# Layer 1's attention with V as the stationary operand and both heads in one bank

## The chip, the cores and the metric

The kernel runs on one core of one Trainium2 chip. The metric is the device time of one execution in microseconds. TensorE is called PE below, VectorE DVE, ScalarE ACT, GpSimdE POOL, SyncE SP (it issues the DMAs).

## The reference

A trunk of two layers on 1024 tokens of 1024 channels, in float32. Layer 0 is differential attention beside a pooling mixer, layer 1 a gated short convolution beside dilated attention; each is followed by a SwiGLU feed-forward block. The change touches layer 1's attention alone. It has 8 heads of 64 channels and three branches of a window and a dilation, whose outputs are combined by their softmax denominators:

```
D_BRANCHES = ((128, 1), (512, 4), (2048, 16))
s = q k^T * 64**-0.5 - slope * distance     # -inf outside window, dilation, causality
o_branch = softmax(s) v ;  lse_branch = m + log(den)
o = sum over branches of softmax(lse)[branch] * o_branch
x = x + concat([conv_part, o]) @ w_out
```

The combined output is the same as one softmax in which a key that lies in several branches counts as often, so the kernel adds one table (the log of the count, or a large negative number) and takes one softmax.

## The kernel before

**Units and tiles.** Layer 1's attention works in 4 units of two heads (m = 0, 1), each over 8 query tiles of 128 tokens (i = 0 to 7), 32 tiles in all, counted by n. Tile i has i + 1 blocks of 128 keys. Per tile and head: PE scores the queries against the keys (`score`, two float32r matmuls for each 512 keys, into PSUM banks 0 and 1 for head 0, 2 and 3 for head 1); DVE adds the bias table while it moves the scores to SBUF, and takes the minimum of the negated sums (`biased`, line 2440); ACT takes the exponential and its sum, the denominator DEN (line 1798); PE transposes the exponentials block by block (`turn`, line 1162) into banks 4 to 6 in turn; ACT copies the first four blocks of the turned map to SBUF and DVE the rest (`turned`, lines 1589 and 2561); PE multiplies the turned map with V (`weigh`, line 1181) into bank 7; DVE multiplies by the reciprocal of the denominator (`denominator`, line 2566, and `scaled`, line 2573) into Y.

In `weigh` the turned map's block (128 keys x 128 queries) is the stationary operand and V's block (128 keys x 64 columns) is moved. The output has 128 queries as partitions and 64 columns. Both heads use the same 64 columns of bank 7, one after the other. The operands are plain float32; most other matmuls are float32r.

**Order.** Each engine has its own instruction list, written out by hand, with semaphores between the lists. For tile n PE runs: turn of head 0, score of head 0 for tile n + 2, weigh of head 0 for tile n - 1, then the same three for head 1. A score waits until DVE has reduced the tile before it in the same banks (`s_mx`), a turn until ACT has taken the exponential (`s_ex`) and a bank of 4 to 6 is free, a weighing until the turned map is copied (`t_ea`, `t_ed`) and bank 7 is free (`o_ok`). DVE runs for tile n: reciprocal of head 0 of tile n - 1, `biased` of head 0 for tile n + 1, reciprocal of head 1, `scaled` of head 1 of tile n - 2, `biased` of head 1, the copy of head 0's turned map, `scaled` of head 0 of tile n - 1, the copy of head 1's turned map. At i = 6 it also builds the two bias tables of the next unit (line 2424).

**After attention.** Y (tokens as partitions) must be turned for the output projection: `turn_y` makes 8 transposes for each of the 4 units (line 1366). They stand between the projection's first tiles (`u_tile`, lines 1083 to 1085, the convolution's half of the channels); ACT and DVE then split the turned Y into high and low float32r parts (`y_hi`, `y_lo`). SP loads three further pieces of the output weights once the last weighing is done (line 805); ACT and DVE split them (`split_o`).

Of the kernel before, what the change touches and what calls it, by code (L numbers as in the profile page):

```python
# [82 lines left out]
def trunk(nc, a, out):  # L83
    ctx = ExitStack()
    with ctx:
# [23 lines left out]
        Y = at("Y", [P, NT, HALF], F32, oA)  # L109
        WOh = at("WOh", [P, 2, D], F32R, oV)  # L110
# [175 lines left out]
        YJ = at("YJ", [P, P], F32, oK + 4 * KB)  # L286

# [75 lines left out]
        o_pe = [sems("o_peA"), sems("o_peB")]  # L363
        o_ok = [sems("o_okA"), sems("o_okB")]
# [90 lines left out]
        def weighed(L, m, n):  # L455

            return bank(7 if n < FILL_FROM and n % 2 else 6)[:, 0:P] if L == 0 else bank(7)[:, 0:HD]
# [128 lines left out]
        def _(sp):  # L586
# [13 lines left out]
            for L in range(2):  # L600
# [479 lines left out]
        def _(pe):  # L1080
# [85 lines left out]
            def weigh(L, m, n):  # L1166

                u, i = n // NT, n % NT
                if n == 0:
                    pe.wait_ge(bank_free[L], 3 * NT)  # L1170
                pe.wait_ge(t_ea[m][L], n + 1)
                if L == 1 and i >= 4:
                    pe.wait_ge(t_ed[m][1], 4 * u + i - 3)
                if L == 0:
                    pe.wait_ge(o_ok[0][0], n + (1 if n < FILL_FROM else 2))
                else:
                    pe.wait_ge(o_ok[1 - m][1], n + 2 + m)
                w, off = (P, u * P) if L == 0 else (HD, u * P + HD * m)
                turned = PTL[m][i % 2] if L else PT[i % 2]
                for j in range(i + 1):  # L1180
                    last = pe.matmul(weighed(L, m, n), turned[:, P * j:P * j + P], V[:, j, off:off + w],  # L1181
                                     start=(j == 0), stop=(j == i))
                last.then_inc(o_pe[m][L], 1)


            for L in range(2):
                for f in (ja_free if L == 0 else []) + [s_mx[0][L], s_mx[1][L]]:
                    pe.sem_inc(f, 1)
                for f in (t_pe[0][L], t_pe[1][L], o_ok[0][L], o_ok[1][L]):
                    pe.sem_inc(f, 2)  # L1190
                pe.sem_inc(od_add[L], 4)
                pe.sem_inc(bank_free[L], NT)
            pe.wait_ge(idn_ok, 4)
            for L in range(2):
# [135 lines left out]
                def out_block(n):  # L1330

                    q, t = n // NT, n % NT
                    if n == 0:
                        pe.wait_ge(uh_lo, 4)

                        pe.wait_ge(o_ok[0][0], 1 + FILL_FROM)
# [7 lines left out]
                    elif n == BLOCKS_IN + 2:  # L1344
                        pe.wait_ge(o_ok[0][0], 2 + TILES0)
# [7 lines left out]
                def turn_y(j):  # L1353
                    if L == 0:
                        pe.wait_ge(y_ok, j + 1)
                        if j < 2:

                            for m in range(2):
                                pe.wait_ge(s_mx[m][0], 1 + TILES0)
                    else:  # L1360
                        pe.wait_ge(o_ok[0][1], 2 + 8 * UNITS)
                        pe.wait_ge(o_ok[1][1], 2 + 8 * UNITS)
                    if j >= 2:
                        pe.wait_ge(yt_lo, 4 * L + j - 1)
# [4 lines left out]
                if L == 0:  # L1369
                    for u in range(UNITS):  # L1370
                        b, g = u % 2, NT * u
                        following = stacks_before(0, u + 1)
                        for i in range(NT):
# [9 lines left out]
                            if g + i > 0:  # L1383
                                weigh(0, 0, g + i - 1)
# [8 lines left out]
                    weigh(0, 0, TILES0 - 1)  # L1393
                else:
                    for u in range(UNITS):
                        b, g = u % 2, NT * u
                        following = stacks_before(1, u + 1)
                        for i in range(NT):
# [3 lines left out]
                            turn(1, 0, u, i)  # L1402
                            if i == NT - 2 and more:
# [5 lines left out]
                            if g + i > 0:  # L1409
                                weigh(1, 0, g + i - 1)  # L1410
# [5 lines left out]
                            if g + i > 0:  # L1416
                                weigh(1, 1, g + i - 1)
                    for m in range(2):
                        weigh(1, m, TILES0 - 1)
# [6 lines left out]
                else:  # L1426
                    pe.wait_ge(uh_lo, 8)
                    pe.wait_ge(wo_lo, WO_AT[1] + 1)
                    for t in range(NT):
                        if t == 1:  # L1430
                            for m in range(2):
                                pe.wait_ge(o_ok[m][1], 2 + TILES0)
# [151 lines left out]
        def _(act):  # L1584
# [124 lines left out]
            for L in range(2):  # L1709
# [135 lines left out]
                def split_o(g):  # L1845
# [3 lines left out]
                    elif g == 1:  # L1849
                        for m in range(2):  # L1850
                            act.wait_ge(o_pe[m][1], 8 * UNITS)
# [13 lines left out]
                def turned(m, g, i):  # L1865
                    act.wait_ge(t_pe[m][L], g + i + 3)
                    if L == 0:
                        if g + i >= 2:
                            act.wait_ge(o_pe[0][0], g + i - 1)
                        w = P * (i + 1)  # L1870
                        src, to = PS[:, 4 * HALF:4 * HALF + w], PT[i % 2]
                    else:
                        w = min(HALF, P * (i + 1))
                        if g + i >= 2:
                            act.wait_ge(o_pe[m][1], g + i - 1)
# [5 lines left out]
                def scaled(n):  # L1881
# [3 lines left out]
                    act.wait_ge(o_pe[0][0], n + 1)  # L1885
                    act.wait_ge(o_ok[0][0], n + 2)
                    nc.scalar.activation(YJ[:], weighed(0, 0, n), ACT.Square, scale=RDN[:, c:c + 1],
                                         accum_out=YSS[:, n:n + 1]).then_inc(y_sq, 1)
                    copy(Y[:, i, P * u:P * u + P], weighed(0, 0, n), scale=RDN[:, c:c + 1]).then_inc(o_ok[0][0], 1)

                def y_hi(j):
                    act.wait_ge(yt_pe, 4 * L + j + 1)
                    kw = dict(scale=SUBG[:, 0:1]) if L == 0 else {}
                    copy(HH[:, (0, 4)[L] + j, :], PS[:, 1024 * (j % 2):1024 * (j % 2) + 1024], **kw).then_inc(yt_hi, 1)
# [8 lines left out]
                if L == 0:  # L1903
                    for n in range(TILES0):
# [15 lines left out]
                        elif n == 12:  # L1920
                            act.wait_ge(o_pe[0][0], NT)
# [208 lines left out]
        def _(dve):  # L2130
# [196 lines left out]
            for L in range(2):  # L2327
# [177 lines left out]
                def y_lo(j):  # L2505
                    dve.wait_ge(yt_hi, 4 * L + j + 1)
                    src, c = PS[:, 1024 * (j % 2):1024 * (j % 2) + 1024], (0, 4)[L] + j
                    if L == 0:
# [4 lines left out]
                        else:  # L2513
                            dve.wait_ge(o_pe[0][0], TILES0 + j - 3)
# [5 lines left out]
                def unit_scaled(u):  # L2520

                    dve.wait_ge(y_rs, u + 1)
                    dve.wait_ge(o_ok[0][0], 2 + NT * (u + 1))
# [4 lines left out]
                if L == 0:  # L2528
                    for n in range(TILES0):
# [11 lines left out]
                        if n >= 4:  # L2541
                            dve.wait_ge(o_ok[0][0], n - 1)
# [10 lines left out]
                else:  # L2553
                    def turned(m, n):
                        u, i = n // NT, n % NT
                        if i >= 4:
                            dve.wait_ge(t_pe[m][1], n + 3)
                            dve.wait_ge(o_pe[m][1], n - 1)
# [16 lines left out]
                    for n in range(TILES0):  # L2575
# [8 lines left out]
                        if n > 0:  # L2584
                            denominator(0, n - 1)
# [13 lines left out]
                        if n > 0:  # L2599
                            scaled(0, n - 1)  # L2600
# [3 lines left out]
                    denominator(0, TILES0 - 1)  # L2604
                    scaled(1, TILES0 - 2)
                    scaled(0, TILES0 - 1)
                    denominator(1, TILES0 - 1)
                    scaled(1, TILES0 - 1)
# [258 lines left out]
```

## Time and profile before

| what | us |
|---|---|
| median of 3 runs | 2194.12 |
| lowest and highest | 2192.97, 2194.75 |
| the profiled execution's span, first to last instruction | 2193.9 |
| layer 1's attention, from its first matmuls to the output projection, counted from the span's start | 1317 to 1455 |
| one of its four units | 33.88 |

The span is the time of the profiled execution from its first to its last instruction; it lies within the three timed runs, and no other time of that execution is given. Times inside it count from its start. In a timeline a row can hold several instructions of the same kind in a row (x10); its length then runs from the start of the first to the modelled end of the last, and the start of the next row shows when the engine could take the next one. A PE pass's modelled end lies well after the start of the pass behind it, since passes overlap.

### The profile page before, as it was taken

To read this page: it belongs to the slowest core of one execution; us is meant where nothing else is said; L and a number is where in the kernel's file an instruction comes from. 1 tells how busy PE (TensorE), PEld (TensorE's weight loads), DVE (VectorE), ACT (ScalarE), POOL (GpSimd) and SP (SyncE) were. 2 spreads that over 40 slices of the span, in tenths; PEclk is the share of its full clock that TensorE was granted. 3 is DMA by queue.
4 is the path that set the end of the run, shared out by engine and by line. 5 is a ranking of instruction groups with operands and counts; after the bars stand their busy time and mean duration, and the time that the engine had idled before them with its cause. 6 is when DMAs were issued, how large, how long until landed. Compare 5 with 4: busy or idle time off the path is not lost.

```text
span 2193.9 us, 30208 instructions
## 1 busy us (share of the span) xinstructions
PE 2156.8 (98%) x10572; PEld 1809.3 (82%) x10572; DVE 1323.6 (60%) x1829; ACT 900.8 (41%) x1497; POOL 860.1 (39%) x563
## 2 busy tenths in 40 slices
PE   8999999999999999999999999999999999999999
PEld 7877798888888887888888888988888888887887
DVE  4345875765555555558597356656765555555555
ACT  4134874443333334435332148642433333334433
POOL 1022442466666672002244133220466777652000
PEclk9999999999999999999999999999999999999999
DMA  5011421055555448674312111311155555557665
GB/s 190 7 59 41 125 78 30 20 183 201 193 190 167 155 152 285 193 244 155 115 39 58 49 58 40 116 39 39 54 195 184 187 179 170 172 172 273 194 195 192
DMA packets 229536, 295.56 MB, mean 135 GB/s; under 512 B 11825, under 2 KB 133169, under 8 KB 229169
## 3 DMA queue, kind: packets, MB, share of 16 engines
q1 hardware_dynamic: 229136, 294.04, 41.0%
q8 instruction: 68, 1.11, 0.2%
q14 instruction: 44, 0.35, 0.1%
q10 hardware_dynamic: 288, 0.05, 0.0%
HBM read 208.06 MB, written 77.59 MB: 130 GB/s over the span
## 4 chain that ended last, share of the span: by engine, by line
PE 81%; issue 13%; DVE 2%; ACT 2%; POOL 2%; DMA 1%; SPq 0%; POOLq 0%; DVEq 0%; ACTq 0%
PE PS L1533 12%; PE PS L1532 12%; PE PS L1531 12%; PE PS L1558 6%; PE PS L1559 6%; PE PS L1560 6%; PE PS L1181 4%; PE PS L1083 4%; PE PS L1085 4%; PE PS L1084 4%; PE PS L1162 2%; POOL QRS L989 1%; PE PS L1137 1%; PE PS L1138 1%; PE PS L1248 1%
## 5 line engine op out<-in xcount | busy, mean ns | idle before, releaser
L2136 DVE TENSOR_TENSOR LINEl<-LINE,HIGH 128x1024 fp32r<-128x1024 f32 x154 | 195.1, 1274 | 167.5 <-ACT HIGH L1589 167.1
L1589 ACT ACTIVATE HIGH<-LINE 128x1024 fp32r<-128x1024 f32 x154 | 163.0, 1060 | 235.8 <-PE PS L1560 209.9
L1558 PE MATMUL PS<-HIGH 128*128 128x512 f32 x616 | 240.3, 390 | 4.4 <-ACT KEEP L1589 4.0
L1560 PE MATMUL PS<-HIGH,LINEl 128*128 128x512 f32 x616 | 239.7, 389 | 0.0
L1559 PE MATMUL PS<-LINEl,HIGH 128*128 128x512 f32 x616 | 239.6, 389 | 0.0
L2136 DVE TENSOR_TENSOR SLOTl<-BLOCKS,RING 128x512 fp32r<-128x512 f32 x168 | 156.0, 929 | 95.3 <-ACT RING L1589 90.7
L921 POOL TENSOR_TENSOR ST<-ST 128x512 f32<-128x512 f32 x132 | 192.5, 1459 | 32.4 <-DMA ST<-in_ffn_w_down 23.8
L1589 ACT ACTIVATE RING<-BLOCKS 128x512 fp32r<-128x512 f32 x168 | 105.9, 630 | 227.2 <-PE PS L1533 223.1
L2136 DVE TENSOR_TENSOR SLOTl<-SLOT,RING 128x512 fp32r<-128x512 f32 x126 | 132.7, 1053 | 88.1 <-ACT RING L1589 87.9
L1558 PEld LDWEIGHTS PS<-HIGH 128*128 128x128 f32 x616 | 115.6, 188 | 29.5 <-DVE LINEl L2136 2.9
L989 POOL TENSOR_TENSOR QRS<-QMS,EXPO 128x8 f32<-128x8 f32 x32 | 52.1, 1638 | 220.8 <-DVE QMS L2397 220.2
L1560 PEld LDWEIGHTS PS<-HIGH,LINEl 128*128 128x128 f32 x616 | 115.6, 188 | 23.9
L1559 PEld LDWEIGHTS PS<-LINEl,HIGH 128*128 128x128 f32 x616 | 115.7, 188 | 23.8
L1589 ACT ACTIVATE RING<-SLOT 128x512 fp32r<-128x512 f32 x126 | 79.2, 630 | 125.5 <-PE PS L1533 115.2
L1531 PE MATMUL PS<-B1h,RING 128*128 128x512 f32 x336 | 130.7, 389 | 0.0
L1532 PE MATMUL PS<-B1l,RING 128*128 128x512 f32 x336 | 130.7, 389 | 0.0
L1533 PE MATMUL PS<-B1h,SLOTl 128*128 128x512 f32 x336 | 130.7, 389 | 0.0
L893 POOL TENSOR_TENSOR SLOT<-BLOCKS 128x512 f32<-128x512 f32 x42 | 55.3, 1316 | 189.8 <-DMA BLOCKS<-in_ffn_w_up 189.8
L926 POOL TENSOR_TENSOR RST<-MSQ,EXPO 128x1 f32<-128x1 f32 x32 | 22.8, 714 | 233.9 <-DVE MSQ L2154 233.9
L1083 PE MATMUL PS<-WQh,HH 128*128 128x512 f32 x256 | 102.5, 400 | 0.6 <-DVE U L2449 0.6
L1085 PE MATMUL PS<-WQh,HL 128*128 128x512 f32 x256 | 99.9, 390 | 0.0
L1084 PE MATMUL PS<-WQl,HH 128*128 128x512 f32 x256 | 99.7, 389 | 0.0
(418 smaller groups left out, 5807.1 us busy)
## 6 DMA issues: line engine op xcount, KB each, us to landing
LINE<-hidden SPq DMA_DIRECT2D x154, 256.0 KB, 2.7
hidden<-HID SPq DMA_DIRECT2D x44, 512.0 KB, 4.4
ST<-in_ffn_w_down SPq DMA_DIRECT2D x44, 512.0 KB, 4.1
sums<-ST SPq DMA_DIRECT2D x22, 1024.0 KB, 6.2
hidden<-ST SPq DMA_DIRECT2D x22, 1024.0 KB, 6.7
LINE<-sums SPq DMA_DIRECT2D x88, 256.0 KB, 2.9
BLOCKS<-in_ffn_w_gate SPq DMA_DIRECT2D x42, 512.0 KB, 4.0
BLOCKS<-in_ffn_w_up SPq DMA_DIRECT2D x42, 512.0 KB, 5.3
```

Of the source, the lines that this page charges most:

```text
L921: nc.gpsimd.tensor_tensor(dst, x, y, op).then_inc(st_sum, 1)
L1083: pe.matmul(dst, lh, rh, start=first, stop=False)
L1084: pe.matmul(dst, lh, rl, start=False, stop=False)
L1085: return pe.matmul(dst, ll, rh, start=False, stop=last)
L1531: pe.matmul(dst, lh, rh[:, k, :], start=k == 0 and not adds_on, stop=False, skip_group_check=adds_on)
L1532: pe.matmul(dst, lh, rl[:, k, :], start=False, stop=False, skip_group_check=adds_on)
L1533: last = pe.matmul(dst, ll, rh[:, k, :], start=False, stop=k == 3, skip_group_check=adds_on)
L1558: pe.matmul(dst, hi[:, 0, ts], hi[:, 1, :], start=j == 0 and not adds_on, stop=False, skip_group_check=adds_on)
L1559: pe.matmul(dst, hi[:, 0, ts], lo[:, 1, :], start=False, stop=False, skip_group_check=adds_on)
L1560: pe.matmul(dst, lo[:, 0, ts], hi[:, 1, :], start=False, stop=j == NJ - 1, skip_group_check=adds_on).then_inc(dn_pe, 1)
L1589: return nc.scalar.activation(dst, src, ACT.Copy, **kw)
L2136: return v.tensor_tensor(dst, src, hi.bitcast(F32), ALU.subtract)
```

## The change

V's block becomes the stationary operand (64 columns) and the turned map is moved (128 queries), so the output has the 64 channels as partitions and 128 queries as columns. Head 0 writes partitions 0 to 63 and head 1 partitions 64 to 127 of the same 128 columns of bank 7; the two heads' matmuls alternate block by block in one function, `weigh_unit`, which stands where head 0's weighing stood. The output is then already turned as the projection needs it: it goes to YT, and layer 1's `turn_y` is gone. The denominators, which belong to queries and so now to columns, must be turned too: DVE takes the reciprocals of both heads' denominators, each repeated over 64 columns (`denominators_by`, 128 x 128 into RB), PE transposes that (`turn_by`, into bank 7's next 128 columns), DVE copies it to SBUF (RS) and multiplies the weighed output by it (`unit_scaled_out`). Semaphores of the two heads' weighings become one. Layer 0 keeps its computation; its functions only lose the argument for the layer.

```diff
+        YT = at("YT", [P, UNITS, TOK], F32, oA)
+        RB = [at(f"RB{b}", [P, P], F32, oK + 4 * KB + 512 * b) for b in range(2)]
+        RS = [at(f"RS{b}", [P, P], F32, oK + 5 * KB + 512 * b) for b in range(2)]
...
+        def unit_out():
+            return bank(7)[:, 0:P]
+        def unit_by():
+            return bank(7)[:, P:2 * P]
...
-                    for m in range(2):
-                        sp.wait_ge(o_pe[m][1], TILES0)
+                    sp.wait_ge(o_pe[1], TILES0)
...
-            def weigh(L, m, n):
...
-                w, off = (P, u * P) if L == 0 else (HD, u * P + HD * m)
-                turned = PTL[m][i % 2] if L else PT[i % 2]
-                for j in range(i + 1):
-                    last = pe.matmul(weighed(L, m, n), turned[:, P * j:P * j + P], V[:, j, off:off + w],
-                                     start=(j == 0), stop=(j == i))
-                last.then_inc(o_pe[m][L], 1)
+            def turn_by(n):
+                if n == 0:
+                    pe.wait_ge(bank_free[1], 3 * NT)
+                pe.wait_ge(o_ok[1], n + 2)
+                pe.wait_ge(rb_ok, n + 1)
+                pe.transpose(unit_by(), RB[n % 2][:], IDN[:])
+
+            def weigh_unit(n):
+                u, i = n // NT, n % NT
+                for m in range(2):
+                    pe.wait_ge(t_ea[m][1], n + 1)
+                    if i >= 4:
+                        pe.wait_ge(t_ed[m][1], 4 * u + i - 3)
+                for j in range(i + 1):
+                    for m in range(2):
+                        off = u * P + HD * m
+                        last = pe.matmul(unit_out()[HD * m:HD * m + HD, :], V[:, j, off:off + HD],
+                                         PTL[m][i % 2][:, P * j:P * j + P], start=(j == 0), stop=(j == i))
+                last.then_inc(o_pe[1], 1)
...
                             turn(1, 0, u, i)
+                            if g + i > 0:
+                                turn_by(g + i - 1)
...
                                 score(1, 0, b, g, i + 2)
                             if g + i > 0:
-                                weigh(1, 0, g + i - 1)
+                                weigh_unit(g + i - 1)
                             turn(1, 1, u, i)
...
                                 score(1, 1, b, g, i + 2)
-                            if g + i > 0:
-                                weigh(1, 1, g + i - 1)
-                    for m in range(2):
-                        weigh(1, m, TILES0 - 1)
+                    turn_by(TILES0 - 1)
+                    weigh_unit(TILES0 - 1)
...
                         u_tile(0, t)
-                        if t in (1, 3, 5, 7):
-                            turn_y(t // 2)
...
                 def y_hi(j):
+                        act.wait_ge(o_ok[1], 2 + NT * (j + 1))
+                        copy(HH[:, 4 + j, :], YT[:, j, :]).then_inc(yt_hi, 1)
...
-                    def denominator(m, n):
-                        c = m + 2 * (n % 2)
-                        dve.wait_ge(s_ex[m][1], n + 1)
-                        att.did(v.reciprocal(RDN[:, c:c + 1], DEN[:, c:c + 1]))
-
-                    def scaled(m, n):
+                    def denominators_by(n):
+                        c = 2 * (n % 2)
+                        for m in range(2):
+                            dve.wait_ge(s_ex[m][1], n + 1)
+                        by = DEN[:, c:c + 2].rearrange("p (m o) -> p m o", o=1).broadcast_to([P, 2, HD])
+                        v.reciprocal(RB[n % 2][:].rearrange("p (m d) -> p m d", d=HD), by).then_inc(rb_ok, 1)
+
+                    def unit_scaled_out(n):
                         u, i = n // NT, n % NT
-                        c, off = m + 2 * (n % 2), u * P + HD * m
-                        att.wait()
-                        dve.wait_ge(o_pe[m][1], n + 1)
-                        v.tensor_scalar(Y[:, i, off:off + HD], weighed(1, m, n), RDN[:, c:c + 1], None, ALU.mult).then_inc(o_ok[m][1], 1)
+                        dve.wait_ge(o_pe[1], n + 1)
+                        att.link(v.tensor_copy(RS[n % 2][:], unit_by()))
+                        v.tensor_tensor(YT[:, u, P * i:P * i + P], unit_out(), RS[n % 2][:], ALU.mult).then_inc(o_ok[1], 1)
...
                         if n > 0:
-                            denominator(0, n - 1)
+                            denominators_by(n - 1)
                         if i == NT - 1:
                             att.wait()
                         if more:
                             biased(0, b, g, i + 1)
-                        if n > 0:
-                            denominator(1, n - 1)
-                        if n > 1:
-                            scaled(1, n - 2)
-                        if more:
                             biased(1, b, g, i + 1)
                         turned(0, n)
...
                         if n > 0:
-                            scaled(0, n - 1)
+                            unit_scaled_out(n - 1)
                         turned(1, n)
```

## Rows read from the trace of the kernel before

**Rows 1.** The page, busy time: us, share of the span, instructions.

```profile
PE 2156.8 (98%) x10572; PEld 1809.3 (82%) x10572; DVE 1323.6 (60%) x1829; ACT 900.8 (41%) x1497; POOL 860.1 (39%) x563
```

**Rows 2.** Busy time by stretch: a unit, the end of attention, the projection's start.

```profile
core 0: us, PE busy (x) PEld busy (x) DVE busy (x) ACT busy (x) POOL busy (x), PEclk, DMA share, GB/s
1349.92:1383.80 33.88, 32.97 (x265) 30.89 (x265) 22.62 (x75) 24.41 (x55) 9.86 (x6) 1.00 0.14 32
...
1452.00:1456.00 4.00, 3.81 (x18) 3.71 (x19) 0.39 (x3) 0.00 (x0) 0.00 (x0) 0.60 0.00 0
1456.00:1460.00 4.00, 4.00 (x11) 3.09 (x10) 0.69 (x1) 0.00 (x0) 0.00 (x0) 0.55 0.75 262
1455.05:1482.61 27.56, 27.56 (x130) 22.89 (x130) 16.38 (x21) 5.00 (x4) 0.00 (x0) 0.92 0.22 77
```

**Rows 3.** Timeline of PE over head 0 of one tile (start, length, instructions).

```profile
1366.98 0.82 PE L1162 MATMUL PS<-IDN,PR 128*128 128x128 f32 x6
1367.56 0.48 PE L1137 MATMUL PS<-K,QST 128*128 128x512 f32 x1
...
1368.57 1.22 PE L1181 MATMUL PS<-V,PT 128*128 128x64 f32 x10
1369.63 0.83 PE L1162 MATMUL PS<-IDN,PR 128*128 128x128 f32 x6
```

**Rows 4.** Instructions of three lines: ns of one, minimum, median and maximum.

```profile
L1277 PE MATMUL PS<-U,PW x16: 591/592/595, 156.5 to 167.9; 128*128 128x512 f32 x16
...
L1366 PE MATMUL PS<-IDN,Y x64: 270/272/273, 346.2 to 1482.6; 128*128 128x128 f32 x64
...
L1181 PE MATMUL PS<-V,PTB x320: 217/275/423, 1323.3 to 1454.9; 128*128 128x64 f32 x160
```

**Rows 5.** Timeline of DVE behind the weighing of Rows 3.

```profile
1369.90 0.28 DVE L2573 TENSOR_SCALAR Y<-PS,RDN 128x64 f32<-128x64 f32 x1 [1.02 <-PE PS L1181]
1370.49 0.42 DVE L2561 COPY PTB<-PS 128x256 f32<-128x256 f32 x1 [0.30 <-PE PS L1162]
1370.83 0.15 DVE L2566 RECIPROCAL RDN<-DEN 128x1 f32<-128x1 f32 x1
1370.90 1.21 DVE L2440 CUSTOM_DVE_ANT_0 PR<-PS,BIAS 128x1024 f32<-128x1024 f32 x1
1372.03 0.09 DVE L2440 DVE_READ_ACCUMULATOR2_ANT NMX<- 128x1 f32 x1
```

**Rows 6.** Instructions of two lines: the reciprocals, of one and two columns.

```profile
L2566 DVE RECIPROCAL RDN<-DEN x64: 152/158/163, 1318.7 to 1452.0; 128x1 f32<-128x1 f32 x64
...
L2482 DVE RECIPROCAL RDN<-DEN x32: 156/160/167, 215.8 to 341.3; 128x2 f32<-128x2 f32 x32
```

**Rows 7.** Groups by line, DVE in the unit of Rows 2: busy us, mean ns, idle before.

```profile
L2573 DVE TENSOR_SCALAR Y<-PS,RDN 128x64 f32<-128x64 f32 x16 | 4.5, 284 | 10.4 <-PE PS L1181 10.3
L2424 DVE SCALAR_TENSOR_TENSOR BIAS<-DIST,SM,MASK 128x1024 f32<-128x1024 f32 x2 | 2.9, 1436 | 0.0
...
L2561 DVE COPY PTB<-PS 128x512 f32<-128x512 f32 x2 | 1.4, 692 | 0.5 <-PE PS L1162 0.5
...
L2561 DVE COPY PT<-PS 128x128 f32<-128x128 f32 x2 | 0.6, 286 | 0.0
L2440 DVE CUSTOM_DVE_ANT_0 PR<-PS,BIAS 128x128 f32<-128x128 f32 x2 | 0.6, 285 | 0.0
```

**Rows 8.** Timeline: a hand-over from DVE to a waiting PE.

```profile
1317.42 0.69 DVE L2418 TENSOR_TENSOR QN<-PS,QRS 128x512 f32<-128x512 f32 x1 [0.72 <-POOL QRS L989]
...
1318.16 0.66 PE L1268 MATMUL PS<-IDN,QN 128*128 128x128 f32 x4 [0.70 <-DVE QN L2418]
```

**Rows 9.** Timeline of PE at the end of attention.

```profile
1446.58 1.04 PE L1162 MATMUL PS<-IDN,PR 128*128 128x128 f32 x8
...
1449.67 1.97 PE L1181 MATMUL PS<-V,PTB 128*128 128x64 f32 x16 [0.54 <-DVE Y L2573]
1452.18 3.11 PE L1181 MATMUL PS<-V,PTB 128*128 128x64 f32 x16 [0.54 <-DVE Y L2573]
```

More of the change, by code:

```diff
@@ L453, in turn_bank, with weighed @@
             return bank(4 + c) if L == 0 else bank(4 + TURNS.index((m, i, c)) % 3)
-        def weighed(L, m, n):
-            return bank(7 if n < FILL_FROM and n % 2 else 6)[:, 0:P] if L == 0 else bank(7)[:, 0:HD]
+        def weighed(n):
+            return bank(7 if n < FILL_FROM and n % 2 else 6)[:, 0:P]
+        def unit_out():
+            return bank(7)[:, 0:P]
+        def unit_by():
+            return bank(7)[:, P:2 * P]
         def block_out(n):
@@ L1164, in turn, with weigh @@
                 last.then_inc(t_pe[m][L], 1)
-            def weigh(L, m, n):
+            def weigh(n):
                 u, i = n // NT, n % NT
                 if n == 0:
[L1170 to L1177, printed above, removed]
-                w, off = (P, u * P) if L == 0 else (HD, u * P + HD * m)
-                turned = PTL[m][i % 2] if L else PT[i % 2]
+                    pe.wait_ge(bank_free[0], 3 * NT)
+                pe.wait_ge(t_ea[0][0], n + 1)
+                pe.wait_ge(o_ok[0], n + (1 if n < FILL_FROM else 2))
                 for j in range(i + 1):
-                    last = pe.matmul(weighed(L, m, n), turned[:, P * j:P * j + P], V[:, j, off:off + w],
+                    last = pe.matmul(weighed(n), PT[i % 2][:, P * j:P * j + P], V[:, j, u * P:u * P + P],
                                      start=(j == 0), stop=(j == i))
-                last.then_inc(o_pe[m][L], 1)
+                last.then_inc(o_pe[0], 1)
+            def turn_by(n):
[16 more added lines that the diff above has]
+                last.then_inc(o_pe[1], 1)
             for L in range(2):
@@ L1188, in _ @@
                     pe.sem_inc(f, 1)
-                for f in (t_pe[0][L], t_pe[1][L], o_ok[0][L], o_ok[1][L]):
+                for f in (t_pe[0][L], t_pe[1][L], o_ok[L]):
                     pe.sem_inc(f, 2)
@@ L1392, in _ @@
                     turn_y(1)
-                    weigh(0, 0, TILES0 - 1)
+                    weigh(TILES0 - 1)
                 else:
@@ L1430, in _ @@
                         if t == 1:
-                            for m in range(2):
-                                pe.wait_ge(o_ok[m][1], 2 + TILES0)
+                            pe.wait_ge(o_ok[1], 2 + TILES0)
                         u_tile(0, t)
-                        if t in (1, 3, 5, 7):
-                            turn_y(t // 2)
                     pe.wait_ge(wo_lo, WO_AT[1] + 2)
@@ L1849, in split_o @@
                     elif g == 1:
-                        for m in range(2):
-                            act.wait_ge(o_pe[m][1], 8 * UNITS)
+                        act.wait_ge(o_pe[1], TILES0)
                     else:
@@ L1884, in scaled @@
                     c = 2 * (i % 4)
[L1885 to L1887 removed]
+                    act.wait_ge(o_pe[0], n + 1)
+                    act.wait_ge(o_ok[0], n + 2)
+                    nc.scalar.activation(YJ[:], weighed(n), ACT.Square, scale=RDN[:, c:c + 1],
                                          accum_out=YSS[:, n:n + 1]).then_inc(y_sq, 1)
[L1889 removed]
+                    copy(Y[:, i, P * u:P * u + P], weighed(n), scale=RDN[:, c:c + 1]).then_inc(o_ok[0], 1)
                 def y_hi(j):
[L1892 to L1894 removed]
+                    if L == 0:
+                        act.wait_ge(yt_pe, j + 1)
+                        copy(HH[:, j, :], PS[:, 1024 * (j % 2):1024 * (j % 2) + 1024], scale=SUBG[:, 0:1]).then_inc(yt_hi, 1)
+                    else:
+                        act.wait_ge(o_ok[1], 2 + NT * (j + 1))
+                        copy(HH[:, 4 + j, :], YT[:, j, :]).then_inc(yt_hi, 1)
                 def score_done():
@@ L2603, in _ @@
                             next_bias(1)
[L2604 to L2608, printed above, removed]
+                    denominators_by(TILES0 - 1)
+                    unit_scaled_out(TILES0 - 1)
                 def split_o(g):
```

41 lines of the change are left out of this document (19 added, 22 removed).

## The prediction

> **What bounds the kernel now.** I read the page's busy times first: PE is busy 98% of the span [rows 1]. Then the busy time by stretch, on layer 1's attention and what follows it: one unit (two heads, eight query tiles) takes 33.88 us, in which PE is busy 32.97, ACT 24.41 and DVE 22.62 [rows 2]. So PE sets the pace of this stage, and the others have about 10 us of room in each unit. Then PE's timeline over one tile [rows 3]: six transposes hold PE 0.58 us, a 1024-key score of one head 1.01 us (0.126 per 128 keys), and the weighing of a tile with five key blocks ten passes in 1.06 us. A plain f32 matmul is thus two passes on the array, and with V's 64 columns moved each pass takes 0.106 to 0.108 us. One unit has 36 blocks for each of two heads, 144 passes, 15.5 us: almost half of PE's time there.
>
> Is that pass bound by moving columns or by loading weights? Another f32 matmul moves 512 columns in passes of 592 ns [rows 4]; a transpose of 128 columns reads 272 ns and a weighing pass of 64 at the least 217, so a moved column costs (592 - 272) / 384 = 0.83 ns, 0.106 us for 128 columns and 0.053 for 64. The old pass moves 64 columns and takes 0.108: it waits for its 128 columns of weights. The new pass loads 64 and moves 128, so it is 0.106 by its moving columns. **Turning the operands round alone gains nothing**; the gain must come from the two halves of the array working at the same time.
>
> **The change part by part.**
>
> *Weighing.* 72 matmuls a unit stay 72, with 144 passes of 0.106. If head 1's passes run beside head 0's, a key block of both heads takes 0.213 us and a unit 7.7 us; if not, 15.3. No row shows two 64-column matmuls side by side, so these are the two ends. I take 7.7, since the two heads alternate block by block and use different partitions of the bank. PE then has 15.5 - 7.7 = 7.8 us a unit less, and one transpose a tile more (eight, 0.9 us): 33.9 would become about 27 if nothing else held it.
>
> *What takes its place: a loop through DVE.* The tile after next can't be scored for head 0 until DVE has reduced the one before it (one pair of PSUM banks per head), PE issues that score ahead of the weighing, and DVE reaches that reduction only after it has scaled the previous tile's weighed output. So weighing, scaling, the copy of the second half of head 1's turned map, the reciprocal, the reduction, the score and the next weighing form a chain that repeats once a tile. Both kernels have it. Before, per unit: hand-over to DVE 0.27 (from PE's next start at 1369.63 to DVE's at 1369.90) x 8 = 2.2; scaling 0.20 x 8 = 1.6 (0.28 less the overlap of 0.08 that successive DVE rows show); copies 1.6 (four, 0.49 on the mean, less overlap) and 0.7 of waits for their transposes; reciprocal 0.07 x 8 = 0.6; reductions 5.3 (0.285 to 1.21 us, mean 0.75, less overlap, x 8); reading the minimum and hand-over to PE (0.09 + 0.05) x 8 = 1.1; scores 36 x 0.126 = 4.5; weighing of head 0 7.7; one bias table 1.2: 26.5 of 33.9 us, hidden under PE [rows 2, 3, 5, 6, 7, 8]. DVE's 10.4 us of waits for weighing are that room [rows 7].
>
> After, per unit:
> - Scaling becomes a copy of the turned reciprocals out of PSUM (128x128, 0.286 by the copy's row), its own hand-over (0.05, as from DVE to PE [rows 8]) and a product (0.29 less 0.08): 0.55 x 8 = 4.4, that is +2.8.
> - The reciprocal of one column becomes one of 128 columns, 64 repeated twice. No row shows a wide reciprocal. At the copy's slope, (692 - 286) / 384 = 1.06 ns per element, it is 0.157 + 127 x 1.06 = 0.29 us. The rows of one and of two columns [rows 6] differ by 3 ns in the mean: 0.54 us. At the most they differ by 15 ns (152 to 167): 2.06 us. I take 0.86 us, 5.5 ns per element, between the mean and the middle of the extremes (7.5), since the mean stands on a single added element: (0.86 - 0.08) x 8 = 6.2, that is +5.6. The ends are 1.7 and 15.8.
> - Switching the array between whole and halves, twice a tile. Below: nothing. Above: the pass in flight must end first, 0.272 - 0.108 = 0.16, and the next be started, 0.05 (as after DVE). I take half, 0.1, for each of eight entries and, through the later transposes, for half of the exits: +1.2 (ends 0 and 2.4).
> - The bias tables of the next unit, 1.44 us each, fall into two neighbouring tiles. The second stays on the chain (1.2); the first now runs longer than the short score and weighing that it runs beside (about 2.9 us of DVE work against 1.7): +1.1.
>
> Sum: 26.5 + 2.8 + 5.6 + 1.2 + 1.1 = 37.2 us a unit against 33.9. The chain is then longer than PE's 27 and sets the pace: +3.3 x 4 = **+13.2 us**.
>
> The page TensorEngine Tiling (Array Packing) of the Trainium skill (section Key Properties) says that a change of tiling mode drains TensorE. By it the switch is at its upper end, the chain 1.2 longer, and the time 5 us more; no row here shows a switch. Half of the chance of the forecast's case lies on that side.
>
> *The end of attention.* Before, from the last transposes to the start of the second part of the output projection: 1446.58 to 1482.61, 36.0 us [rows 2, 9]. In it head 0's and head 1's last weighings follow each other with waits of 0.54, the granted clock is 0.60 and 0.55 in the two stretches from 1452 to 1460 (it falls from 2.4 to 1.2 GHz there, after those waits), and the 32 transposes of Y (3.5) stand between the projection's tiles. The projection's 96 matmuls alone are 27.56 - 3.5 - 2.2 (the half clock) = 21.9. After: transposes 0.86, hand-over and copy 0.27 + 0.69, reciprocal 0.86, its turn 0.1, one weighing 1.7 to 1.9, 4.8 in all; then 21.9; and DVE, which frees the projection's banks, has y_lo(0) and split_o(1) in front (3072 elements at 1.06, 3.2 us) without PE's transposes to cover them: I count half, 1.6. Together 28.3, 7.7 less; if the clock falls as before (3 us) 4.7. I take **-6.3**. y_hi no longer waits for PE; SP's three loads and their waits keep their order, and nothing is queued behind a new wait there. PE's new waits (for the reciprocal, for bank 7) have behind them the score and the weighing, which is the chain above. ACT needs 24.4 us a unit and stays hidden.
>
> Sum: 2193.9 (the profiled span, inside the three runs of 2192.97 to 2194.75, median 2194.12) + 13.2 - 6.3 = **2201 us**.
>
> **The rivals.**
> 1. *The wide reciprocal is as cheap as a copy* (0.29 to 0.45 us) and the switch is free. For it: other DVE rows grow by about 1 ns per element. Then the unit is 37.2 - 4.5 - 1.2 = 31.5 us, -9.6 in four, and the end gives 8: 2176, up to 2187 with 0.45 us and some switching. It decides below 0.5 us of reciprocal. This is the case that ends faster.
> 2. *The halves don't overlap*, or 64 columns of weights load no faster than 128: the change doesn't do what it says. Weighing is 15.3 us a unit and lies on the chain: 37.2 + 7.6 = 44.8, +44 in four, 2232; with the cheap reciprocal 2214. Against it only the issue order speaks.
> 3. *The reciprocal costs at least 7.5 ns per element*, the middle of the extremes: 1.11 us or more, +2 us a unit and +8 in all, 2209 to 2215. For it: the extremes lean upwards. Against it: the mean of 3 ns.
>
> The page VectorE: DVE Perf Modes of the Trainium skill (section First, the fixed hardware budget) says that a reciprocal divides iteratively with a repeat count of 8. By eight times the copy's slope an estimate is 1.22 us and the time 2212: this rival. The 3 ns of our rows don't agree with it, but they are one element.
>
> **How the numbers follow.** About 0.2%, 4.4 us, is what these runs can tell from no change. Chances: the forecast's case 0.33 (own range 2190 to 2212: 0.03 faster, 0.12 within, 0.18 slower), rival 1 0.29, rival 2 0.24, rival 3 0.14. Faster 0.29 + 0.03 = 0.32; same 0.12; slower 0.18 + 0.24 + 0.14 = 0.56. The range 2176 to 2234 goes from rival 1's lower end to just past rival 2's upper one, and leaves out longer reciprocals together with halves that don't overlap.
>
> **What would show it.** The weighing's sixteen pass pairs of a last tile should start 1.7 us apart from first to last (3.4 would be rival 2). The reciprocal's row should read 0.86 us (0.3: rival 1; over 1.1: rival 3). DVE's waits for weighing should shrink from 10.4 us a unit while PE shows idle time before its scores or its turn of the reciprocals, and PE's busy share of the unit should fall well below 32.97 of 33.88. A unit should take about 37 us. The forecast is wrong if the chain is not the one that PE waits for (ACT's copies instead), or if PE, now idle in every tile, is granted the lower clock inside attention: 12 us of scores and weighings a unit would then double.

## The result, and the profile after

The changed kernel takes 2204.81 us (median of 4 runs, 2202.9 to 2206.96) against 2193.55 (2192.46 to 2194.75): ratio 1.005, 95% interval 1.0036 to 1.0064, 11 us slower. The forecast was 2201, slower. The profiled execution has a span of 2201.1 us (its own time is 2202.9, so 1.8 us lie around the span), 7.2 more than before's 2193.9.

The page's busy times, answering to [rows 1], show little: PE works 17 us less and DVE 20 more.

```profile
PE 2140.1 (97%) x10572; PEld 1775.0 (81%) x10572; DVE 1343.7 (61%) x1797; ACT 902.2 (41%) x1497; POOL 861.0 (39%) x563
```

The busy time by stretch, for the unit that answers to the one of [rows 2]:

```profile
core 0: us, PE busy (x) PEld busy (x) DVE busy (x) ACT busy (x) POOL busy (x), PEclk, DMA share, GB/s
...
1355.02:1392.84 37.82, 30.71 (x273) 24.00 (x272) 27.98 (x66) 24.75 (x55) 9.87 (x6) 1.00 0.12 29
```

A unit takes 37.82 us where it took 33.88. PE was busy in all but 0.9 us of a unit; now it is idle for 7.1, and no engine fills the unit. That is what a loop through several engines looks like. The waits of PE and of DVE in that unit name its two ends (total, times, longest):

```profile
PE PS L1195 <- DVE RB L2589: 4.7, 4, 2.0
PE PS L1148 <- DVE NMX L2461: 2.2, 5, 0.7
```

```profile
DVE RS L2594 <- PE PS L1207: 8.9, 7, 2.3
DVE PTB L2582 <- PE PS L1173: 0.6, 2, 0.4
```

PE waits for the reciprocal (`turn_by`, L1195) and for the reductions (`score`, L1148), and DVE waits for the weighing (L1207). DVE's groups by line in the same unit, answering to [rows 6, 7]:

```profile
L2589 DVE RECIPROCAL RB<-DEN 128x128 f32<-128x128 f32 x8 | 7.5, 942 | 0.0
...
L2595 DVE TENSOR_TENSOR YT<-PS,RS 128x128 f32<-128x128 f32 x8 | 2.3, 291 | 0.3
L2594 DVE COPY RS<-PS 128x128 f32<-128x128 f32 x8 | 2.3, 290 | 8.9 <-PE PS L1207 8.9
```

One turn of the loop can be read off the two timelines. First DVE, answering to [rows 5] (the weighed tile is scaled, and the same for the next tile at 1377.65):

```profile
1372.31 0.29 DVE L2594 COPY RS<-PS 128x128 f32<-128x128 f32 x1 [1.13 <-PE PS L1207]
1372.64 0.29 DVE L2595 TENSOR_TENSOR YT<-PS,RS 128x128 f32<-128x128 f32 x1
1373.00 0.29 DVE L2582 COPY PT<-PS 128x128 f32<-128x128 f32 x1
1373.21 0.94 DVE L2589 RECIPROCAL RB<-DEN 128x128 f32<-128x128 f32 x1
1374.07 1.03 DVE L2461 CUSTOM_DVE_ANT_0 PR<-PS,BIAS 128x896 f32<-128x896 f32 x1
1375.02 0.08 DVE L2461 DVE_READ_ACCUMULATOR2_ANT NMX<- 128x1 f32 x1
...
1377.65 0.29 DVE L2594 COPY RS<-PS 128x128 f32<-128x128 f32 x1 [1.20 <-PE PS L1207]
```

Then PE, answering to [rows 3]:

```profile
1374.30 0.30 PE L1195 MATMUL PS<-IDN,RB 128*128 128x128 f32 x1
1375.16 0.50 PE L1148 MATMUL PS<-K,QST 128*128 128x512 f32 x1 [0.56 <-DVE NMX L2461]
1375.49 0.40 PE L1149 MATMUL PS<-K,QST 128*128 128x512 f32 x1
1375.73 0.40 PE L1148 MATMUL PS<-K,QST 128*128 128x512 f32 x1
1375.96 0.40 PE L1149 MATMUL PS<-K,QST 128*128 128x512 f32 x1
1376.29 1.31 PE L1207 MATMUL PS<-PT,V 128*64 128x128 f32 x20
1377.53 0.88 PE L1173 MATMUL PS<-IDN,PR 128*128 128x128 f32 x6
```

From 1372.31: scaling and a wait for the next transposes 0.69, copy 0.21, reciprocal 0.86, reduction with its minimum about 1.03, hand-over to PE 0.06, score 1.13, weighing 1.24, hand-over to DVE 0.12: 5.34 us, and at 1377.65 it begins anew. Every step starts when the one before it ends. The two weighings of this turn start 5.12 us apart; before, the same two started 4.63 apart (the second is in [rows 3], the first of each pair here, after and before):

```profile
1371.17 1.09 PE L1207 MATMUL PS<-PTB,V 128*64 128x128 f32 x16
```

```profile
1363.94 1.00 PE L1181 MATMUL PS<-V,PTB 128*128 128x64 f32 x8
```

The end of attention, PE's timeline from the last transposes, answering to [rows 9]:

```profile
1462.10 1.09 PE L1173 MATMUL PS<-IDN,PR 128*128 128x128 f32 x8
1464.92 0.30 PE L1195 MATMUL PS<-IDN,RB 128*128 128x128 f32 x1 [1.73 <-DVE RB L2589]
1465.16 1.97 PE L1207 MATMUL PS<-PTB,V 128*64 128x128 f32 x32
1467.06 0.50 PE L1094 MATMUL PS<-WOh,UH 128*128 128x512 f32 x1
...
1479.52 0.50 PE L1094 MATMUL PS<-WOh,UH 128*128 128x512 f32 x1 [1.26 <-DVE X L2346]
...
1490.53 0.39 PE L1094 MATMUL PS<-WOh,UH 128*128 128x512 f32 x1
```

From the last transposes to the projection's second part (1490.53) are 28.4 us; before they were 36.0.

**Where the 7.2 us of the span come from.** From the first score (at 1314.3 before) to the last transposes 132.3 us became 148.9 (+16.6: the middle units +3.9 each, the stretch up to the first unit's last weighing +6.2, the last unit's part +2.6). The end gives 7.6 back (3.2 of them by the clock, below), the projection's second part 0.8. The rest is spread: the first score starts 1.1 us earlier, although nothing was changed ahead of it. Such differences between executions are not the change's: over the runs below, the identical part behind the projection's first half takes from 687.9 to 691.3 us. So the verdicts below go by ratios and by the length of a unit, not by single spans.

**The clock.** In the +6.2 of the first unit a stretch shows a lower granted clock (by stretch, the columns as above; the first row is the stretch before):

```profile
1346.00:1349.00 3.00, 1.35 (x15) 1.24 (x17) 2.47 (x7) 1.03 (x4) 0.00 (x0) 0.92 0.00 0
1349.00:1352.00 3.00, 3.00 (x25) 2.67 (x22) 0.58 (x2) 0.00 (x0) 0.00 (x0) 0.51 0.00 0
```

The same weighing there, and one unit later:

```profile
1348.15 2.95 PE L1207 MATMUL PS<-PT,V 128*64 128x128 f32 x28
...
1387.59 1.75 PE L1207 MATMUL PS<-PT,V 128*64 128x128 f32 x28
```

After a stretch in which PE was busy for 1.35 of 3.00 us the clock is at 1.2 GHz for some 3 us. From that weighing to the next are 6.87 us instead of 5.25: 1.6 us. Such a stretch does not always lower the clock: in the next two units and at the end of attention PE is busy for 1.40, 1.09 and 1.27 of 3.00 us (from 1385.50, 1423.00 and 1462.00), and the clock stays at 1.00. What decides it is not shown.

The profiled execution of the kernel before has a dip too, at the end of attention [rows 2]. Experiment 4 below has the same end without a dip, and there the stretch from the last transposes to the projection's second part (1457.19 to 1489.97) takes 32.8 us instead of 36.0. So 3.2 of the 7.6 us that the end gives back are the clock of one execution, and 4.4 the change's own. The profiled execution of the changed kernel is the one of the four with the highest mean clock (0.999 and 2202.9 us; the others 0.997 and 0.998, 2204.7 to 2207.0). So more such dips in the other executions would account for the median's lying 1.9 above it; there is no trace of them, so this is argued, not shown.

### The profile page after: what moved, and what is told of

Same layout as the page of the kernel before. It is cut to its first block, busy times and chain, and to the rows that moved or that the text cites. A ratio compares the mean times of both kernels' runs of the same rounds, so it can differ in the third digit from the quotient of the medians.

```text
span 2201.1 us, 30153 instructions
## 1 busy us (share of the span) xinstructions
PE 2140.1 (97%) x10572; PEld 1775.0 (81%) x10572; DVE 1343.7 (61%) x1797; ACT 902.2 (41%) x1497; POOL 861.0 (39%) x563
## 3 DMA queue, kind: packets, MB, share of 16 engines
q8 instruction: 68, 1.11, 0.2%
## 4 chain that ended last, share of the span: by engine, by line
PE 77%; issue 13%; DVE 4%; ACT 2%; POOL 2%; DMA 1%; SPq 0%; POOLq 0%; DVEq 0%; ACTq 0%
PE PS L1551 12%; PE PS L1552 12%; PE PS L1550 12%; PE PS L1577 6%; PE PS L1578 6%; PE PS L1579 6%; PE PS L1094 4%; PE PS L1096 4%; PE PS L1095 4%; PE PS L1207 1%; POOL QRS L1000 1%; PE PS L1274 1%; PE PS L1272 1%; PE PS L1273 1%; PE PS L1148 1%
## 5 line engine op out<-in xcount | busy, mean ns | idle before, releaser
L1817 ACT ACTIVATE PR<-PR,NMX 128x256 f32<-128x256 f32 (+7 forms) x128 | 98.5, 774 | 9.4 <-DVE NMX L2461 9.1
```

The source lines that it names most:

```text
L1817: nc.scalar.activation(pr, pr, ACT.Exp, bias=NMX[:, c:c + 1], scale=-1.0, accum_out=DEN[:, c:c + 1]).then_inc(s_ex[m][L], 1)
```

## The experiments

They ran on three chips (1 to 4, 5 to 8, and 9 and 10), each time beside the kernel before, whose median there was 2195.4 to 2196.4. Times are given as ratios to it; the changed kernel's is 1.005.

**1. The reciprocal of two columns**, spread over the partitions by PE.

```diff
-                pe.transpose(unit_by(), RB[n % 2][:], IDN[:])
+                c = 2 * (n % 2)
+                for m in range(2):
+                    pe.matmul(unit_by()[HD * m:HD * m + HD, :], RDN[:, c + m:c + m + 1].broadcast_to([P, HD]), IDN[:], start=True, stop=True)
...
-                        v.reciprocal(RB[n % 2][:].rearrange("p (m d) -> p m d", d=HD), by).then_inc(rb_ok, 1)
+                        v.reciprocal(RDN[:, c:c + 2], DEN[:, c:c + 2]).then_inc(rb_ok, 1)
```

> The reciprocal takes two columns instead of 128; PE spreads each over 64 partitions by reading the column 64 times as stationary operand. Loop theory (every DVE instruction between the scaling and head 0's next reduction is added to each tile): the reciprocal falls from 0.94 to about 0.16 us, 0.78 less for each of 8 tiles, so a unit falls from 37.8 to about 31.6 us and the kernel by 25 us, to about 2180 (2177 to 2186, PE's own 29 to 30 us a unit being the floor). Rival (PE itself needs the 37.8 us: switching between whole and halves, and the clock): within 3 us of the changed kernel's 2204.8. Rival (DVE's total work is the bound, 28.0 us busy a unit plus hand-overs): also about 2180.

Measured: 2192.75 us, ratio 0.999 (0.9981 to 1.0), 13 us less than the changed kernel, half of what was expected; a unit 34.21 us where about 31.6 was expected. The busy time of that unit and PE's two waits in it:

```profile
1387.28:1421.49 34.21, 31.74 (x298) 24.62 (x297) 22.84 (x66) 24.56 (x54) 9.89 (x6) 1.00 0.40 128
```

```profile
1416.05 0.44 PE L1197 MATMUL PS<-IDN,RDN 128*64 128x128 f32 x4 [1.76 <-DVE RDN L2590]
...
1420.57 0.44 PE L1197 MATMUL PS<-IDN,RDN 128*64 128x128 f32 x4 [0.60 <-DVE RDN L2590]
```

The reciprocal was on the loop: 0.27 to 0.75 us came off in seven of the eight tiles. But then PE's own 31.7 us show, and 2.4 us of waits in the two tiles where DVE builds the next unit's bias tables. The rival that PE needs 37.8 falls.

**2. One head after the other** in the weighing.

```diff
-                for j in range(i + 1):
-                    for m in range(2):
+                for m in range(2):
+                    for j in range(i + 1):
```

> All of head 0's matmuls of a weighing first, then all of head 1's; the work is the same. If two neighbouring matmuls of different halves run at the same time, as the passes 0.055 us apart suggest, the overlap is lost: a weighing of eight blocks takes 3.5 us instead of 1.97, a unit 7.6 us more, the kernel 30 us more, about 2235. Rival (a pass with 64 columns of weights is short by itself, whichever half the one before used): no change, 2205.

Measured: 2221.15 us, ratio 1.0116 (1.0099 to 1.0132), 14 us more than the changed kernel; a unit 42.13 us, 4.3 more. PE's weighings of eight blocks (with what follows), of two and of four:

```profile
1400.41 3.33 PE L1207 MATMUL PS<-PTB,V 128*64 128x128 f32 x32
1403.67 0.33 PE L1173 MATMUL PS<-IDN,PR 128*128 128x128 f32 x1
...
1409.79 0.67 PE L1207 MATMUL PS<-PTB,V 128*64 128x128 f32 x8
...
1418.18 1.58 PE L1207 MATMUL PS<-PTB,V 128*64 128x128 f32 x16
```

On the mean the 32 passes start (3.33 - 0.27) / 31 = 0.099 us apart, against (1.97 - 0.27) / 31 = 0.055 with the heads alternating. The same passes, the same weights, so the rival falls. But 0.099 is the mean of two spacings. The starts of the single passes, which the rows merge, lie 0.109 us apart in the trace, except for eight in the middle, on the mean 0.055 apart; by the two long first passes of 0.32 us these are the last four of head 0 and the first four of head 1, side by side. With the heads alternating the passes start in pairs, 0.007 us apart, and a pair every 0.109. So a pass takes 0.109 us either way (0.106 was predicted), and two run at the same time when they are in different halves. This also is why the price was half of the expected: a weighing of two blocks has four passes a head, all of which still meet (0.67 us against 0.66), and each pass beyond eight costs 0.055 more (four blocks 1.58 us against 1.09), for 84 of the 144 passes of a unit. That is 4.6 us, and 4.3 were measured; the tile with the tables grew less, since PE waited there for 1.5 us instead of 2.0.

**3. The reciprocal later.** Wide as before, behind both reductions on DVE; its turn on PE behind the weighing; DEN with four slots.

```diff
-                        if n > 0:
-                            denominators_by(n - 1)
...
                             biased(0, b, g, i + 1)
                             biased(1, b, g, i + 1)
+                        if n > 0:
+                            denominators_by(n - 1)
...
-                            if g + i > 0:
-                                turn_by(g + i - 1)
...
                                 weigh_unit(g + i - 1)
+                                turn_by(g + i - 1)
```

> The wide reciprocal stays, but moves on DVE from ahead of head 0's reduction to behind head 1's, and its turn on PE from ahead of the score to behind the weighing (DEN has four slots instead of two). Loop theory: the reciprocal leaves the path from the scaling to the next score, and a unit falls to 30 to 33 us, where PE's own work or DVE's whole list is the next bound: 2177 to 2190. Rival (DVE's total work is the bound): no gain, 2202 to 2207. Rival (PE's own time): no gain either.

Measured: 2192.35 us, ratio 0.9982 (0.9972 to 0.9992), a unit 33.97 us: as much as making it short, though short of the expected 30 to 33 and 2177 to 2190. PE still waits 3.0 us of that unit for reductions. DVE is busy for 28.2 us of that unit, as in the changed kernel (27.98). So it was not the amount of DVE's work.

**4. The kernel before with a wide reciprocal** added.

```diff
                             denominator(0, n - 1)
+                            by = DEN[:, 2 * ((n - 1) % 2):2 * ((n - 1) % 2) + 1].rearrange("p (m o) -> p m o", o=1).broadcast_to([P, 1, P])
+                            att.did(v.reciprocal(RB[:].rearrange("p (m d) -> p m d", d=P), by))
```

> The kernel before, with one 128x128 reciprocal a tile added on DVE ahead of head 0's reduction, its output not read. Loop theory: 0.86 us a tile is 6.9 us a unit, the loop of before was worked out at 26.5 of 33.9 us, so 33.4 still hides under PE, except where the bias tables stand: 0 to 2 us a unit, 2194 to 2202. Rival (a longer DVE list delays PE at once): 2215 to 2222.

Measured: 2207.63 us, ratio 1.0051 (1.0035 to 1.0068), 12 us more than before; a unit 36.71, +2.8 where 0 to 2 was expected; the time lies between the two expectations. The room of 7.4 us that the prediction found is a sum over unequal tiles. PE's rows of two short tiles show where it is missing:

```profile
1396.53 0.50 PE L1138 MATMUL PS<-K,QX 128*128 128x512 f32 x1 [0.64 <-DVE NMX L2441]
...
1399.93 0.50 PE L1138 MATMUL PS<-K,QX 128*128 128x512 f32 x1 [0.20 <-DVE NMX L2441]
```

The tiles of one and two blocks and the one with the tables grow by 0.8, 0.5 and 0.75 us, the others by 0.24 at the most.

**5. Both: short and late.** PE's turn of the reciprocal then shares the weighing's halves.

> Both edits together: the two-column reciprocal spread by PE, behind head 1's reduction on DVE, and its turn right behind the weighing, so that it shares the weighing's two switches of the array instead of having two of its own. Theory (with the reciprocal gone from the loop, PE's own work is the bound, and each entry into the halves costs 0.1 us, each exit 0.16): the unit of the first experiment, 34.2 us with 31.75 busy, loses 8 x 0.26 = 2.1 us: 32.1, the kernel 8 us less than there, 2184 to 2187. Rival (DVE's loop is still the bound, the switches cost nothing): as the first and the third experiment, 2190 to 2194.

Measured: 2190.73 us, ratio 0.9975 (0.9966 to 0.9984): 3 us less than the first experiment, 8 were expected. Inconclusive on the switches by its time: one of its units has a clock dip (35.4 against 33.8), and PE waits 3.3 us of a unit for reductions, which the first did not.

**6. The tables apart**, on top of it, and **7. the same move alone** in the changed kernel.

```diff
                             biased(0, b, g, i + 1)
+                            if i == NT - 1:
+                                bias(1, 1 - b, 2 * u + 3)
+                                att.wait()
                             biased(1, b, g, i + 1)
...
-                        if i == NT - 2 and u + 1 < UNITS:
-                            next_bias(1)
```

> The same, with head 1's bias table of the next unit built one tile later, between head 0's and head 1's reductions, so that no longer both tables stand ahead of head 0's short reduction. Theory (the waits of 2 to 2.4 us a unit that PE has left are those for the two tables): three units lose 1.3 to 2 us each, 4 to 6 us less than the fifth experiment, 2179 to 2182. Rival (the tables only move the wait to head 1's reduction): as the fifth.

> The changed kernel with nothing but that move of head 1's table. Loop theory: PE's two longest waits, 2.0 and 1.4 us for the turn of the reciprocal, lose up to 1.3 us a unit in three units: 2200 to 2203 against 2204.8 (on this chip's scale about 1 more). Rival (no effect on the loop): no change.

Measured: the sixth 2185.98 us, ratio 0.9957 (0.9945 to 0.997), a unit 32.50: 4 us less than the fifth, the lower end of what was expected. PE is busy for 30.43 of a unit, as in the fifth, and 1.3 less than in the first experiment, for eight pairs of switches less; busy time runs to the modelled ends of passes and so holds part of a switch, and this is not its price. The seventh 2200.77, ratio 1.0024 (1.0015 to 1.0033), a unit 36.62 instead of 37.82: 1.2 us a unit, just the second table. The ratio says 6 us in all, of which three units explain 3.6.

**8. The transposes of Y put back** into the projection of the changed kernel.

```diff
                         u_tile(0, t)
+                        if t in (1, 3, 5, 7):
+                            j = t // 2
...
+                            for k in range(NT):
+                                pe.transpose(PS[:, 1024 * (j % 2) + P * k:1024 * (j % 2) + P * k + P], YT[:, j, P * k:P * k + P], IDN[:])
```

> The changed kernel with the 32 transposes of layer 1's output put back between the projection's tiles, 8 of them behind each second tile as before; nothing reads what they write. By the prediction's step for the end of attention: their own 3.5 us less the 1.26 us that PE waits there for DVE without them, 2 to 3.5 us more than the changed kernel. Rival (the projection waits for something else, the transposes were hidden): no change.

Measured: 2208.41 us, ratio 1.0061 (1.0046 to 1.0076), 2.4 us more than the changed kernel's 1.005; the two intervals overlap, so the time alone does not settle it. The stretch from the projection's first matmul to its first one on HH does: 47.3 us, against 45.2, +2.1, the transposes less the wait for DVE that they cover.

**9. The weighing ahead of the score**, in the changed kernel: one swap on PE.

```diff
                                 turn_by(g + i - 1)
+                            if g + i > 0:
+                                weigh_unit(g + i - 1)
...
                                 score(1, 0, b, g, i + 2)
-
-                            if g + i > 0:
-                                weigh_unit(g + i - 1)
```

> The changed kernel, wide reciprocal and all, with one swap on PE: the weighing (behind the turn of the reciprocal) goes ahead of head 0's next score instead of behind it. Loop theory: score and reduction leave the loop, which shrinks to scaling, copy, reciprocal, turn and weighing, 0.55 + 0.21 + 0.86 + 0.15 + 0.1 + about 1.1 + 0.27 = 3.2 us a tile, under PE's own 30.7 / 8 = 3.8; a unit falls from 37.8 to 31 to 33 us, the kernel to 2180 to 2190, without a nanosecond of DVE's work removed. Rival (the wide reciprocal's time on DVE is the cost as such): no change, 2203 to 2207.

Measured: 2191.98 us, ratio 0.9988 (0.9978 to 0.9997), 14 us less than the changed kernel, with DVE's list untouched; a unit 34.15 us (the one before it 35.65, at a mean clock of 0.95). The rival falls, since the whole loss is gone while the reciprocal stays. PE's remaining waits in that unit (the row also counts the wait of 1.39 just before it; 4.8 lie inside), and the two longest:

```profile
PE PS L1195 <- DVE RB L2588: 6.1, 4, 2.9
```

```profile
1416.73 0.30 PE L1195 MATMUL PS<-IDN,RB 128*128 128x128 f32 x1 [2.94 <-DVE RB L2588]
1421.76 0.30 PE L1195 MATMUL PS<-IDN,RB 128*128 128x128 f32 x1 [1.39 <-DVE RB L2588]
```

All of them are for the wide reciprocal, so it is not free in this order either. The two longest stand in the tiles with the tables; that these are why the expected 2180 to 2190 was missed by 2 us is argued, as no run moves the tables alone in this order.

**10. The sixth with this swap.**

> The sixth experiment (narrow reciprocal behind the reductions, one entry into the halves, tables apart) with the same swap: the weighing ahead of the score. Loop theory: PE's remaining waits for reductions, 2.6 us a unit, vanish and PE's own 30 us are the bound: unit 32.5 to 30, the kernel 7 to 9 us less than the sixth, 2177 to 2180. Rival (those waits come from DVE's whole list): as the sixth, 2186.

Measured: 2180.11 us, ratio 0.9929 (0.9916 to 0.9942): 16 us faster than the kernel before, 6 less than the sixth (7 to 9 were expected; a unit stays 1.5 above the 30). The unit's busy times and PE's waits:

```profile
1379.10:1410.55 31.45, 29.92 (x296) 24.86 (x297) 23.43 (x67) 24.33 (x56) 9.89 (x6) 1.00 0.38 126
```

```profile
PE PS L1210 <- DVE PT L2583: 0.8, 1, 0.8
PE PS L1210 <- DVE PTB L2583: 0.5, 1, 0.5
PE PS L1194 <- DVE RDN L2589: 0.2, 1, 0.2
```

No reduction is waited for any more; what is left is DVE's copy of the turned map, 1.5 us in a unit. PE's own 30 us are the bound. A second place for the weighed output, so that scaling could lag behind by a tile, was not tried.

## Why the prediction came out right, step by step

- **Weighing.** A pair of passes takes 0.109 us, 0.106 predicted, and the sixteen pairs of a last tile start 1.7 us apart from first to last, as forecast. The halves do overlap, for long weighings only because the heads alternate (experiment 2). Rival 2 is out. The rule of the Trainium skill that tiles operate independently (TensorEngine Tiling (Array Packing), Key Properties) agrees with the two passes in 0.109 us.
- **The loop.** The forecast's mechanism, step for step, with 5.34 us in the tile shown. The experiments cut it in three places (shorter, experiment 1; moved, 3; its order changed, 9), each for 13 to 15 us. One of its signs was weak: DVE's waits for weighing fell only from 10.4 to 8.9 us a unit, since that wait is itself a part of the loop.
- **Its terms.** Scaling: copy to product 0.33 and product to the next row 0.21, 0.54 for 0.55. Reciprocal: 0.942 us, 0.86 predicted; between starts 0.86 for 0.78, +0.6 us a unit. That is (942 - 158) / 127 = 6.2 ns per added element; the 0.29 to 0.45 of rival 1, the 1.11 of rival 3 and the upper end of 2.06 are out. The estimate of 1.22 us from the repeat count of the Trainium skill (VectorE: DVE Perf Modes, First, the fixed hardware budget) does not agree with the 0.942.
- **The switch** was set too low, above all for PE. Behind a 512-column pass the next starts 0.23 us later; the weighing starts 0.33 after the one at 1375.96: 0.10 to enter. Its last pass, counted at the same 0.055, is over at about 1377.38 (1376.29 + 20 x 0.0545), and the transposes start at 1377.53: 0.15 to leave. Eight pairs are 2.0 us of PE's time a unit, for which the prediction had nothing. On the loop it counted eight entries and four exits as 1.2; at these prices they are 1.4. The Trainium skill's rule that a change of mode drains the array (TensorEngine Tiling (Array Packing), Key Properties) agrees in that it costs at all; the 0.25 of a pair lies between the prediction's middle of 0.2 and its upper end of 0.4.
- **A unit**: 37.8 us for 37.2 (two terms low by 0.6 and 0.2, the others together high by some 0.2). First score to last transposes +16.6, of which 1.6 by the clock, for +13.2.
- **The end**: from the last transposes to the second part 28.4 us for 28.3, so 7.6 less; the -6.3 allowed for a falling clock, which stayed at 1.00. But this agreement has luck in it: the 36.0 that it starts from held a dip of the clock, and against an end without one (experiment 4) the change is worth 4.4. Experiment 8 shows 2.1 of that for the transposes. The parts that the prediction lists as 4.8 add up to 4.5 to 4.7; 5.0 were measured (1462.10 to 1467.06). The wait for DVE without PE's transposes was 1.26 us for 1.6.
- **Mis-sized, though it did not decide: the numbers for the other cases.** Rival 1 put a unit without the wide reciprocal at 31.5 us and the kernel at 2176 to 2187. Experiment 1 gives 34.2 and 2193, and experiments 4 and 9 show the same flaw: the chain was summed over a unit and set against PE's sum, but each tile has its own longer side. The tiles with tables stay on DVE's list whatever else gets shorter. And PE's own work is 30 us, not 27: 2 for the switches were counted on the chain only, and the rest is not broken down.
- **The time**: the span of 2201.1 meets the sum's 2201, but partly by chance: 1.8 us around the span were left out, and each of the two profiled executions has a dip of the clock, before's worth 3.2 us and after's 1.6. Without the dips the +7.2 would be about +8.8, an estimate from these figures. Against the medians the change is +11.3, predicted +6.9: the loop cost more (15.0 for 13.2 without the dip), and the end gave less (4.4 for 6.3).

## What to carry to other kernels

When every engine has idle time and a stage still gets longer, look for a loop: follow one tile through all its engines until the same row comes again, and add up. What counts is whether an operation lies on that loop, not how long its engine works; before making an operation cheaper, see whether the step behind it can be issued in another order (here one swap of two calls was worth as much as removing 83% of the reciprocal's time). Compare chain and bound tile by tile; sums over unequal tiles hide both waits and room.

## What was not expected of the hardware

Passes of 64 columns of weights and 128 moved columns start 0.109 us apart in the same half; in alternating halves two start 0.007 apart, a pair every 0.109. With all of head 0's passes listed first, its last four and head 1's first four still ran side by side, by their starts in experiment 2. Entering the halves cost 0.10 us, leaving them 0.15. A stationary operand may be one column read 64 times: four such passes spread two reciprocals over 128 partitions, and PE's next score started 0.37 us after their start (1390.13 and 1390.50 in experiment 1), for the 0.94 us that DVE needed for the wide reciprocal.
